# Scan order: four steps of each scan group moved one slot, and the last group's turn moved from slot 9 to slot 10

## What is computed

```
xbc = silu(conv(xbc) + conv_b);  xs, B, C = split(xbc)
a_cs = cumsum(dt * a) within a chunk
decay = exp(a_cs[l] - a_cs[s]) for l >= s
y_diag = (C B^T * decay) @ (xs * dt)
state  = B^T @ (decay_to_the_end * xs * dt)
y_off  = exp(a_cs) * (C @ state of the chunk before)
y = (y_diag + y_off + ssm_d * xs) * silu(z)
y = y * rsqrt(mean(y*y over its group of 512) + eps) * ssm_norm_w
```

## Time and profile before

| | before |
|---|---|
| median of three runs | 2053.12 us |
| the profiled execution's own time | 2053.77 us |
| its span, first to last instruction | 2052.0 us |
| PE busy | 2032.3 us, 99% |
| DVE busy | 1344.0 us, 66% |
| ACT busy | 1024.0 us, 50% |
| POOL busy | 202.6 us, 10% |
| mean granted TensorE clock | 0.997 |

### The profile page before, as it was taken

One profiled execution on the slowest core, in us unless ns is written; L12 is line 12 of the kernel. 1 busy time (PEld: TensorE's weight loads), 2 busy tenths in 40 slices (PEclk: granted clock), 3 DMA queues, 4 the chain that ended last, 5 costly groups with the idle time before them and its releaser, 6 DMA issues.

```text
span 2052.0 us, 26419 instructions
## 1 busy us (share of the span) xinstructions
PE 2032.3 (99%) x9394; PEld 1681.8 (82%) x9394; DVE 1344.0 (66%) x1623; ACT 1024.0 (50%) x1437; POOL 202.6 (10%) x362
## 2 busy tenths in 40 slices
PE   9999999999999999999999999999999999999997
PEld 7888888888888878888888888888888888888886
DVE  6755676676665677775677767666546656655664
ACT  5444545554543466664566644554434434434443
POOL 4000010101010011110011110100001000000000
PEclk9999999999999999999999999999999999999999
DMA  8756565656657666666666667766666666766664
GB/s 274 216 166 194 168 200 159 202 168 200 175 176 234 186 187 195 193 194 210 182 182 195 194 226 239 225 208 222 209 193 204 223 196 190 229 200 182 224 214 134
DMA packets 201765, 408.85 MB, mean 199 GB/s; under 512 B 14945, under 2 KB 15041, under 8 KB 200241
## 3 DMA queue, kind: packets, MB, share of 16 engines
q1 hardware_dynamic: 188656, 364.56, 57.4%
q0 software_dynamic: 12816, 42.34, 7.0%
q10 hardware_dynamic: 176, 0.40, 0.1%
HBM read 379.91 MB, written 2.16 MB: 186 GB/s over the span
## 4 chain that ended last, share of the span: by engine, by line
PE 90%; DVE 3%; issue 2%; ACT 2%; DMA 1%; DVEq 1%; ACTq 0%; POOL 0%; POOLq 0%; SPq 0%
PE acc L299 28%; PE acc L301 28%; PE acc L300 28%; DVE lo L266 1%; PE x L945 1%; PE tr L334 1%; PE x L885 1%; PE tr L902 1%; ACT hi L260 1%; DMA GA<-x 0%; ACT W L1208 0%; PE x L892 0%; PE x L817 0%; PE tr L904 0%; PE tr L907 0%
## 5 line engine op out<-in xcount | busy, mean ns | idle before, releaser
L266 DVE TENSOR_TENSOR lo<-raw,hi 128x1024 fp32r<-128x1024 f32 x688 | 835.7, 1229 | 505.5 <-ACT hi L260 499.8
L260 ACT ACTIVATE hi<-raw 128x1024 fp32r<-128x1024 f32 x688 | 717.9, 1056 | 614.1 <-PE acc L301 559.6
L299 PE MATMUL acc<-hi,LAh 128*128 128x512 f32 x1840 | 730.0, 397 | 2.2 <-DVE lo L266 2.1
L301 PE MATMUL acc<-hi,LAl 128*128 128x512 f32 x1840 | 717.3, 390 | 0.0
L300 PE MATMUL acc<-lo,LAh 128*128 128x512 f32 x1840 | 716.7, 390 | 0.0
L299 PEld LDWEIGHTS acc<-hi,LAh 128*128 128x128 f32 x1840 | 345.6, 188 | 78.9 <-DVE lo L266 6.2
L301 PEld LDWEIGHTS acc<-hi,LAl 128*128 128x128 f32 x1840 | 345.4, 188 | 72.5
L300 PEld LDWEIGHTS acc<-lo,LAh 128*128 128x128 f32 x1840 | 345.7, 188 | 71.2 <-issue 1.4
L299 PE MATMUL acc<-hi,LBh 128*128 128x512 f32 x896 | 350.6, 391 | 0.0
L300 PE MATMUL acc<-lo,LBh 128*128 128x512 f32 x896 | 349.2, 390 | 0.0
L301 PE MATMUL acc<-hi,LBl 128*128 128x512 f32 x896 | 349.1, 390 | 0.0
(11 more groups left out here) (308 smaller groups left out, 1237.2 us busy)
## 6 DMA issues: line engine op xcount, KB each, us to landing
raw<-w_in SPq DMA_DIRECT2D x304, 512.0 KB, 4.0
raw<-w_up SPq DMA_DIRECT2D x128, 512.0 KB, 4.1
raw<-w_down SPq DMA_DIRECT2D x128, 512.0 KB, 4.8
raw<-w_proj_ssm SPq DMA_DIRECT2D x64, 512.0 KB, 4.2
raw<-w_proj_nsa SPq DMA_DIRECT2D x32, 512.0 KB, 4.4
raw<-w_out SPq DMA_DIRECT2D x32, 512.0 KB, 5.6
W<-acs_rows POOLq DMA_DIRECT2D x8, 1024.0 KB, 4.9
W<-TB POOLq DMA_DIRECT2D x48, 128.0 KB, 4.2
```

Of the source, the lines that this page charges most:

```text
L260: act.activation(hi[:, sl, :, :], raw[:, sl, :, :], ACT.Copy).then_inc(s_hi, 1)
L266: dve.tensor_tensor(lo[:, sl, :, :], raw[:, sl, :, :], hi[:, sl, :, :].bitcast(F32), ALU.subtract).then_inc(s_lo, 1)
L299: pe.matmul(o, xh, wh, start=(k == 0), stop=False)
L301: x = pe.matmul(o, xl, wh, start=False, stop=(k == KT - 1))
```

## The change

In the scan iterations PE's first product, second product and turn of the gated rows stand one slot sooner (5, 7, 11). DVE's decay products stand in slots 2 and 3, its reading of the products in 5 and 7, and its split in slot 12 behind conv_out, so ahead of turn_rows (slot 13) and no longer behind it. In slot 7 the take of the first chunk now stands ahead of scan_y1. ACT's token_rows stands in slot 1, behind the split of the fifth group and ahead of scan_exp, and its scan_split in slot 11. In group 7 the new map gives PE slots 0, 4, 5, 6 and 10; ACT slots 1, 1, 2, 4, 7, 8 and 10; and DVE slots 0, 1, 2, 3, 5, 6 and 10. Conv, squares and norm on ACT stay in slots 8, 9 and 10. No instruction is added or removed.

```diff
         def last_hooks(hooks):
 
-            last = {6: 5, 8: 6, 9: 7, 10: 8, 12: 9, 13: 9}
+            last = {7: 6, 9: 7, 10: 8, 11: 10, 12: 10}
             return {last.get(s, s): h for s, h in hooks.items()}
...
             def scan_hooks(g):
-                return {0: [lambda: scan_cb(g)], 4: [lambda: scan_state(g)], 6: [lambda: scan_y0(g)],
-                        8: [lambda: scan_y1(g)], 12: [lambda: scan_turn_y(g)]}
+                return {0: [lambda: scan_cb(g)], 4: [lambda: scan_state(g)], 5: [lambda: scan_y0(g)],
+                        7: [lambda: scan_y1(g)], 11: [lambda: scan_turn_y(g)]}
...
             def scan_hooks(g, k0):
-                return {0: [lambda: token_rows(g)], 1: [lambda: scan_exp(g, 0)], 2: [lambda: scan_exp(g, 1)], 4: [lambda: scan_state(g)], 9: [lambda: scan_squares(g)],
-                        10: [lambda: scan_norm(g)], 12: [lambda: scan_split(g, k0)]}
+                return {1: [lambda: token_rows(g), lambda: scan_exp(g, 0)], 2: [lambda: scan_exp(g, 1)], 4: [lambda: scan_state(g)], 9: [lambda: scan_squares(g)],
+                        10: [lambda: scan_norm(g)], 11: [lambda: scan_split(g, k0)]}
...
             def scan_hooks(g, k0):
                 return {0: [lambda: scan_first(g)], 1: [lambda: scan_inputs(g)],
-                        3: [lambda: scan_w(g, 0)], 4: [lambda: scan_w(g, 1)], 6: [lambda: scan_y0(g)], 8: [lambda: scan_y1(g)],
-                        13: [lambda: scan_split(g, k0)]}
+                        2: [lambda: scan_w(g, 0)], 3: [lambda: scan_w(g, 1)], 5: [lambda: scan_y0(g)], 7: [lambda: scan_y1(g)],
+                        12: [lambda: scan_split(g, k0)]}
...
             def scan_iteration(C, par, m, xa, g=None, k0=None):
                 hk = scan_hooks(g, k0) if g is not None else {}
-                hk[7] = hk.get(7, []) + [lambda: take(C, par, XR[:, 1, :], xa + 1)]
+                hk[7] = [lambda: take(C, par, XR[:, 1, :], xa + 1)] + hk.get(7, [])
...
-                hk[12] = [lambda: conv_out(m, XC[:, :, :])]
-                hk[13] = [lambda: turn_rows(m)] + hk.get(13, [])
+                hk[12] = [lambda: conv_out(m, XC[:, :, :])] + hk.get(12, [])
+                hk[13] = [lambda: turn_rows(m)]
...
             hk = last_hooks(scan_hooks(7, 12))
-            hk[13] = hk.get(13, []) + [lambda: merge(0, 8 * C_PB2 + 14)]
-            hk[14] = hk.get(14, []) + [lambda: turn_merged(0)]
+            hk[13] = [lambda: merge(0, 8 * C_PB2 + 14)]
+            hk[14] = [lambda: turn_merged(0)]
```

## The result

The changed kernel took 2060.61 us (median of 11 runs, 2059.14 to 2061.05) against 2053.41 us of the kernel before (11 runs, 2051.84 to 2056.83). The ratio is 1.0034, with a 95% interval of 1.0026 to 1.0042. That is slower beyond the noise, and 0.3 us above the forecast range of 2052.3 to 2060.3. The forecast was 2056.7 and "the same".

What follows compares the result with a forecast made beforehand. PE, 99% busy, was taken to bound the kernel. The terms -0.8 - 0.3 + 7.1 + 0.8 - 3.0 - 0.9 = +2.9 us on 2053.77 gave 2056.7 us, range 2052.3 to 2060.3.

Steps and rivals of the forecast that it cites:

- What bounds the kernel: Whole kernel: PE, 99% busy, sets the time with its waits; only 4.1 us of waits behind the start.
- The turn: Seven scan groups beside a conv: PE's turn waits 1.02 us for ACT's norm in each, a cost of 7.1 us.
- the other six groups repeat these distances: Turn in groups beside a conv: the others wait like the one read, 1.02 us, bounds 0.9 and 1.1 each.
- Moves that I cost at nothing: Moved DVE, ACT, POOL and SP steps, with turn_rows some 1.6 us later: no cost, rows may land 1.1 us later.
- The slack: After a late turn PE is 1.0 us later, covering a 0.1 to 0.2 us wait for the state's copy.
- First group: First scan group: late lo go, 1.6 us, but PE waits 0.7 to 0.8 for the state's copy; gain 0.8 us.
- Fourth group: Fourth scan group: its late lo before the sixth group is covered by PE's later turn; gain 0.3 us.
- Last group: Last scan group: waits for decay products and norm go, and the half clock with them; gain 3.9 us.
- The rival that it keeps a wait: Last group: state's copy or a late lo replaces the decay products, up to 3.0 us stay, 2059.7 us; 15%.
- More breaks: PE's stream: one more group behind a product in seven iterations, 0.12 us each; cost 0.8 us, bounds 0 and 1.
- The rival of half clock behind the turns: The 1.0 us turn waits lower the granted clock, 1.6 us a fall; all seven give 2068 us; 8%.
- Against the median: Total: +2.9 us against the profiled execution of 2053.77, +3.6 us or 0.17% against the median of the runs.

Runs made afterwards that it cites:

- experiment 5: Kernel before, with the last group's decay products in DVE slots 2 and 3, its turn and splits in slot 10, and token_rows in slot 1 everywhere: 2049.91 us.
- experiment 1: Changed kernel with PE's turn and ACT's split back in slot 12, DVE's split in 13 behind turn_rows, last group kept in slot 10: 2050.83 us.
- experiment 2: Changed kernel with only DVE's split moved back behind turn_rows (slot 13), PE's turn still in slot 11: 2056.98 us, ratio 1.0020.
- the last set: Last of three sets of runs: the changed kernel took 2059.83 us in it, the kernel before 2052.4 us.
- Experiment 6: Kernel before with only PE's turn of the gated rows and ACT's split moved to slot 11, last group as before: 2057.97 us, ratio 1.0028.
- experiment 7: Changed kernel with ACT's squares ahead of the conv in slot 8: 2069.74 us (four runs), ratio 1.0087.
- 10: Changed kernel, unchanged, profiled once more: 2059.83 us, ratio 1.0030.
- experiment 4: Kernel before with the last group alone changed: decay products in DVE slots 2 and 3, turn and splits in slot 10: 2050.23 us, ratio 0.9989.

## Why the prediction was wrong, point by point

The medians lay the difference out in one chain, each step one part of the change:

| kernel | us | step |
|---|---|---|
| before | 2053.0 | |
| experiment 5: last group, token_rows | 2049.9 | -3.1 |
| experiment 1: products and decay products sooner too, the take ahead of the second | 2050.8 | +0.9 |
| experiment 2: PE's turn and ACT's split in slot 11 too | 2057.0 | +6.2 |
| changed: DVE's split ahead of turn_rows too | 2060.6 | +3.6 |

The last step is +2.9 us with the changed kernel's 2059.8 of the last set. The rows of the chain come from different sets, in which the kernel before moved by up to 1 us.

- **What bounds the kernel: right.** PE's busy time moved by 0.5 us, and the rest of the difference is waiting.
- **The turn: right in mechanism and size.** Seven waits were forecast at 7.1 us in starts. The trace has 7.4 us in starts, 6.3 by modelled ends. Six are 1.0 us each. The third is 1.4, because ACT's hi behind the conv waits 0.66 us there and the norm starts 9.1 us after the turn of XR instead of 8.7. The trace of the kernel before has that too, so "the other six groups repeat these distances" was not quite so. Experiment 6 has the waits without any other part of the change, and experiment 7 shows the cause, the place of the squares.
- **"Moves that I cost at nothing": this step failed.** The prediction saw that turn_rows comes 1.6 us later and wrote that the rows "may now land 1.1 us later without harm". Both numbers stood side by side and did not fit, and the 0.5 us between them got no term. The rows also took 1.5 us longer to land in the median, for which I had no term at all. ACT waits 9.2 us for them, PE loses 2.8 us up to the first product and 3.6 up to its end, where 0.8 was forecast, and experiment 2 gives 2.9 to 3.6 us for the order on DVE.
- **The slack: right, but spent twice.** The 1.0 us that the late turn lends is real (experiment 6). The 0.1 to 0.2 us of the state's copy that it was to cover can be read as well: from state product to the turn of XR most groups take 16.28 us with the late turn and rows on time (experiment 2), and 16.4 without the late turn (experiment 1). In the changed kernel the slack had to cover the late rows as well.
- **First group: right.** The late lo went, and a wait for the copied state came: 0.7 us was forecast; the first product lost 0.1 us in this trace and 0.6, 0.8 and 0.6 in those of experiments 1, 2 and 10. The small loss of the first trace is chance.
- **Fourth group: its wait changed its name.** The gain of 0.3 us did not come in the changed kernel. The late lo is gone, and the first product lost 0.4 us for the copied state. With the rows on time PE's late turn does cover it, as forecast (experiments 2 and 6 lose nothing there).
- **Last group: the decay products and the clock right, the rest too high.** The rival that it keeps a wait came true in part. It lost 0.9 us at the copied state, which the rival names, but by late rows, which it does not. With the rows on time the gain of 3.9 us is there between the two profiled executions (2053.77 and 2049.89 in experiment 4). Between the medians it is 2.8 us; why it is smaller there no run shows.
- **More breaks: about right.** Where nothing waits, it takes 16.28 us from state product to turn of XR in experiment 2 and 16.19 in experiment 6, where both products stand in their old slots. That is 0.09 us for a break, 0.6 in seven groups against 0.8 forecast. The +0.9 us in the chain also holds the waits for the state of experiment 1, and its scatter is as large.
- **The rival of half clock behind the turns: did not come.** All windows of 5 us around turn waits have a clock of 1.00, in every profile.
- **Against the median.** The forecast of the profiled execution was 3.1 us too low. 3.6 - 0.8 = 2.8 us of it lie at the first product, the step that failed. The turns took 0.3 us more than forecast, and what is left is within a few tenths.

## What to carry to other kernels

Before a step is moved one slot sooner, follow its inputs back to the first step that is not moved; if that leaves less room than a slot, the move is a wait in every iteration, whatever else becomes ready sooner. When two hooks change places on a busy engine, look for a DMA behind the one that moves back, and give it two terms, one for the later issue and one for what it meets when it is issued: here some 1.5 us of later issue came with 1.5 us of longer landing. Slack that a new wait lends to other engines counts once; write down which late step it is spent on.

## What the runs showed of the hardware

The spread of the turned rows (four DMAs of 128 KB from POOL) had a median landing of 2.8 us in all eight profiles in which turn_rows stands ahead of the split, and of 4.2 to 4.4 us in the four in which the split stands ahead of it. The shortest landing was 2.5 to 2.6 us in all of them. In the third, sixth and seventh group of the changed kernel the spread moved beside weight loads (0.3 to 0.4 MB of the one and 1.1 to 1.2 of the other in 5 us), while before most of it (0.4 of 0.5 MB) moved when the weights' queue moved 0.1 MB in 3 us.

The fall of the granted clock is not a matter of the wait's length alone. In two profiles of the kernel before it fell after waits of 1.25 and 1.46 us (by modelled ends) for the decay products. In experiment 7 it fell once, and another time it did not, after a wait that was longer:

```profile
837.30 2.67 PE L945 MATMUL x<-XDT,W 128*128 128x64 f32 x16 [1.39 <-ACT XCT L1214]
...
1192.97 2.00 PE L945 MATMUL x<-XDT,W 128*128 128x64 f32 x16 [1.58 <-ACT XCT L1214]
```
```profile
840.00:845.00 5.00, 5.00 (x19) 4.04 (x19) 2.38 (x4) 1.06 (x1) 0.00 (x0) 0.82 0.92 289
...
1190.00:1195.00 5.00, 3.42 (x24) 2.84 (x23) 3.48 (x4) 4.81 (x6) 0.00 (x0) 1.00 0.45 144
```

The same sixteen products took 2.67 us with the fall and 2.00 us without. In the scan groups of all twelve profiles there are three falls, all behind waits ahead of these 64-column products. There is none at the turn waits, which are seven or eight to a profile where the turn stands in slot 11, and up to 1.3 us long. What decides between the two places stays open.
